# A second layer of experts in pairs of 64 rows instead of one by one with 128

## The reference, cut to what matters

```python
def moe_ffn(h, w_router, e_bias, w_gate, w_up, w_down, s_gate, s_up, s_down):
    scores = jax.nn.sigmoid(h @ w_router)                  # 64 experts
    _, idx = lax.top_k(scores + e_bias, 8)                 # 8 per token
    wts = jnp.take_along_axis(scores, idx, axis=-1)
    wts = wts / wts.sum(-1, keepdims=True) * 2.5
    ...
    # for each expert e, over the tokens that chose it:
    a = jax.nn.silu(xb @ w_gate[e]) * (xb @ w_up[e])       # 1024 -> 256
    y = a @ w_down[e]                                      # 256 -> 1024
    ...
    return routed + (jax.nn.silu(h @ s_gate) * (h @ s_up)) @ s_down
```

## Time and profile before

| | |
|---|---|
| median of 3 runs | 3581.51 us (3578.46 to 3589.11) |
| span of the profiled execution | 3580.4 us |
| its own time | not listed apart; the median is 1.1 us over the span |
| PE busy | 3395.6 us, 95% |
| DVE, ACT, POOL busy | 79%, 43%, 19% |
| mean granted TensorE clock | 0.979 of 2.4 GHz |
| traffic | 799.48 MB, mean 223 GB/s |
| second layer's experts | from about 2884 us to 3525 us of the span |

### The profile page before, as it was taken

The page is one execution under the profiler, slowest core; times in us unless marked ns, Lnnn a source line. Parts: engine busy times, 40 slices in busy tenths (PEclk is TensorE's granted clock), DMA queues, the critical chain, the costliest instruction groups (busy, mean ns, idle before and its releaser), DMA issues.

```text
span 3580.4 us, 55190 instructions
## 1 busy us (share of the span) xinstructions
PE 3395.6 (95%) x22040; PEld 2848.9 (80%) x22040; DVE 2823.8 (79%) x3225; ACT 1553.3 (43%) x2135; POOL 666.3 (19%) x437
## 2 busy tenths in 40 slices
PE   8998899999997999999899999999899899999997
PEld 8996689999995799997556777777687777777776
DVE  7877777888877777976668888888674688888885
ACT  1013323000014232011334888888432468888883
POOL 0001100101002000100002444443100024444430
PEclk9999999999998999999999999999999999999999
DMA  6545333554545344541026999999742279999993
GB/s 238 188 168 212 142 130 142 189 189 179 185 160 213 120 156 161 188 154 71 24 94 219 384 380 370 368 370 380 276 192 106 83 264 347 350 353 343 348 352 145
DMA packets 121585, 799.48 MB, mean 223 GB/s; under 512 B 34016, under 2 KB 36064, under 8 KB 51680
## 3 DMA queue, kind: packets, MB, share of 16 engines
q1 hardware_dynamic: 80208, 735.14, 55.1%
q0 software_dynamic: 39024, 59.61, 4.7%
q10 hardware_dynamic: 2080, 1.05, 0.1%
HBM read 808.77 MB, written 71.83 MB: 246 GB/s over the span
## 4 chain that ended last, share of the span: by engine, by line
PE 80%; DVE 14%; ACT 3%; DMA 2%; issue 1%; SPq 0%; DVEq 0%; POOL 0%; ACTq 0%; POOLq 0%
PE ps L453 75%; PE ps L472 4%; DVE ring_r L400 2%; DVE ring_r L399 1%; DVE ring_r L418 1%; DMA ring<-yd_dram 1%; DVE ring L1391 1%; DVE arena L2339 1%; DMA arena<-yd_dram 1%; DVE arena L1264 0%; DVE arena L1242 0%; ACT arena L1504 0%; ACT ring_r L412 0%; DVE arena L1221 0%; DVE arena L1249 0%
## 5 line engine op out<-in xcount | busy, mean ns | idle before, releaser
L453 PE MATMUL ps<-arena_r,ring_r 128*128 128x256 f32 (+1 forms) x9776 | 1278.9, 289 | 36.9 <-DVE ring_r L400 16.0
L453 PEld LDWEIGHTS ps<-arena_r,ring_r 128*128 128x128 f32 x9776 | 1218.0, 190 | 73.2 <-DVE ring_r L400 16.1
L453 PE MATMUL ps<-ring_r,arena_r 128*128 128x512 f32 (+1 forms) x2906 | 805.8, 392 | 1.3 <-DVE arena_r L2208 0.9
L453 PEld LDWEIGHTS ps<-ring_r,arena_r 128*128 128x128 f32 x2906 | 527.6, 189 | 113.7 <-DVE arena_r L2208 1.3
L453 PE MATMUL ps<-arena_hi,arena_r 128*128 128x512 f32 x1540 | 507.8, 397 | 4.7 <-DVE ring_r L2941 4.7
L400 DVE TENSOR_TENSOR ring_r<-ring,ring_r 128x4096 fp32r<-128x4096 f32 (+2 forms) x104 | 445.4, 4283 | 3.6
L3057 POOL DMA_INDIRECT yd_dram<-arena,small x129 | 229.7, 1781 | 727.4 <-PE ps L472 643.1
L453 PEld LDWEIGHTS ps<-arena_hi,arena_r 128*128 128x128 f32 x1540 | 290.1, 188 | 69.5 <-DVE ring_r L2941 5.1
L2916 DVE TENSOR_TENSOR ring_r<-ring,ring_r 128x2048 fp32r<-128x2048 f32 x130 | 298.0, 2292 | 22.8 <-ACT ring_r L2980 15.7
L2916 DVE TENSOR_TENSOR ring_r<-ring,arena_hi 128x2048 fp32r<-128x2048 f32 x128 | 293.5, 2293 | 24.3 <-ACT arena_hi L2980 17.5
L3049 POOL DMA_INDIRECT arena<-xd_dram,small x129 | 272.8, 2114 | 151.3 <-DVE arena L2737 60.7
(11 more groups left out here) (350 smaller groups left out, 3539.9 us busy)
## 6 DMA issues: line engine op xcount, KB each, us to landing
ring<-wexp_dram SPq DMA_DIRECT2D x387, 1024.0 KB, 8.8
ring<-stream_dram SPq DMA_DIRECT2D x143, 2048.0 KB, 7.8
ring<-yd_dram SPq DMA_DIRECT2D x5, 2048.0 KB, 12.7
arena<-yd_dram SPq DMA_DIRECT2D x3, 2048.0 KB, 13.4
arena<-yd_dram SPq DMA_DIRECT2D x8, 512.0 KB, 6.3
ring<-yd_dram SPq DMA_DIRECT2D x8, 512.0 KB, 9.4
xd_dram<-arena POOLq DMA_DIRECT2D x6, 512.0 KB, 6.0
consts_sb<-consts_dram SPq DMA_DIRECT2D x1, 2242.0 KB, 16.2
```

The costliest lines, as they stand in the source:

```text
L453: return pe.e.matmul(ps, lhsT=lhsT, rhs=rhs, start=start, stop=stop, skip_group_check=True)
```

## The change

Layer 1's experts are taken two at a time with 64 slots each. Blocks are now 64 slots (`SLOTS[1] = 64`), section 0 is blocks 0 to 66, always computed (64 experts and up to three second blocks), which is 33 pairs and a single block.

- The weights are no longer split: hidden and down layers are plain fp32 matmuls with a stationary operand of 64 columns, expert h of the pair in array columns 64h to 64h + 63 and PSUM rows 64h to 64h + 63 of one bank. The loops alternate h.
- Rows are not fetched from DRAM. `h` is kept in SBUF by token, as high and low parts (`HTH`, `HTL`), and PE multiplies them with a one-hot matrix of slots (`OHG`): for a group of four blocks 8 chunks x 2 token halves x 2 parts, of 256 columns (`pe_gather`), which comes out already turned.
- Results do not go to DRAM. They are scaled by their slot's weight, split into high and low (`PYH`, `PYL`), and PE multiplies them with the turned one-hot matrix (`OHT`) and adds them up in the four banks `routed`, on top of the shared expert's output, over all pairs (`combine`: 8 chunks x 2 parts, of 256 columns).
- The list of tokens, the indirect DMAs of POOL, the copies into `yd`, and the loads and sums of the combine are gone for this layer. The blocks past 64 are listed by DVE during the first three pairs (`dve_extra_experts`, `dve_extra_slots`).
- There are ten weight buffers (`NPAIR`); the issue points are six, two, then `shared`.
- Within a pair's step PE runs `hidden(j)`, `down(j-1)`, 2 transposes, half a group's gather, 2 transposes of the one-hot matrix, `combine(j-1)`. These use four banks in turn (4 to 7).

```diff
-SLOTS = {0: 128, 1: 128}
-SECTIONS = {0: ((0, 65), (65, 68), (68, 96)), 1: ((0, 64), (64, 65), (65, 68), (68, 80))}
+SLOTS = {0: 128, 1: 64}
+SECTIONS = {0: ((0, 65), (65, 68), (68, 96)), 1: ((0, 67), (67, 71), (71, 96))}
 NBLK = 96
 NRAW = 8
+NPAIR = 10
...
+        class Pairs:
...
+                self.pairs = [(b, min(2, b1 - b)) for b in range(b0, b1, 2)]
+                self.groups = [(b, min(4, b1 - b)) for b in range(b0, b1, 4)]
...
+                for j in range(len(self.pairs) + 1):
+                    if j < len(self.pairs):
+                        self.items += [(part, j, h) for part in "ab" for h in range(self.pairs[j][1])]
+                    if j:
+                        self.items += [("d", j - 1, h) for h in range(self.pairs[j - 1][1])]
...
+        def pe_gather(pe, S, g, quarters):
+            K, n = S.key, 64 * S.groups[g][1]
+            for c2 in quarters:
+                ps = take(pe, K, "gather", g, c2)
+                for c in (2 * c2, 2 * c2 + 1):
+                    o = 256 * (c % 2)
+                    for tk in range(2):
+                        for i, part in enumerate((HTH, HTL)):
+                            pe.wait_ge(*at("rows low", tk, c // 4))
+                            pe.wait_ge(*at(K, "onehot", g))
+                            ins = mm(pe, ps[:, o:o + n], as_r(part.v(1024 * tk + 128 * c, 128)), onehot(OHG, g, tk, n, True),
+                                     tk == 0 and i == 0, tk == 1 and i == 1)
+                ins.then_inc(*pe.mark("ps", K, "gather", g, c2))
+        def pe_pairs(pe, S):
+            K, np_, ng = S.key, len(S.pairs), len(S.groups)
+            pe.banks, pe.taken = range(4, 8), 0
+            if S.b0:
...
+            def hidden(j):
+                ps = take(pe, K, "hidden", j)
+                for k in range(KT):
+                    part = "a" if k < 4 else "b"
+                    for h in range(S.pairs[j][1]):
+                        pe.wait_ge(*at("left", K, "gather", j // 2, k // 2))
+                        pe.wait_ge(*S.got(part, j, h))
+                        ins = mm(pe, ps[64 * h:64 * h + 64, :], gathered(j // 2, k, 128 * (j % 2) + 64 * h, 64),
+                                 S.raw(part, j, h)[:, col(k % 4, 512)], k == 0, k == KT - 1)
+                        if k % 4 == 3:
+                            ins.then_inc(*pe.mark(K, "used", part, j))
+                pe.here("ps", K, "hidden", j)
+            def down(j):
+                for nn in range(2):
+                    ps = take(pe, K, "y", j, nn)
+                    for k in range(2):
+                        for h in range(S.pairs[j][1]):
+                            o = 1024 * k + 512 * nn
+                            pe.wait_ge(*at("left", K, "h", j))
+                            pe.wait_ge(*S.got("d", j, h))
+                            ins = mm(pe, ps[64 * h:64 * h + 64, :], PAT[j % 2].v(128 * k + 64 * h, 64), S.raw("d", j, h)[:, o:o + 512],
+                                     k == 0, k == 1)
+                            if k == 1:
+                                ins.then_inc(*pe.mark("ps", K, "y", j, nn))
+                pe.here(K, "used", "d", j)
+            def turn_hidden(j):
+                P_ = 64 * S.pairs[j][1]
+                ps = take(pe, K, "h", j)
+                for k in range(2):
+                    pe.wait_ge(*at("left", K, "hidden", j))
+                    ins = tr(pe, ps[:, 128 * k:128 * k + P_], PSUM_.v(128 * k, 128)[0:P_, :], P_)
+                ins.then_inc(*pe.mark("ps", K, "h", j))
...
+            def turn_onehot(j):
+                P_ = 64 * S.pairs[j][1]
+                ps = take(pe, K, "w", j)
+                for tk in range(2):
+                    pe.wait_ge(*at(K, "onehot", j // 2))
+                    ins = tr(pe, ps[0:P_, col(tk)], OHW[j // 2 % 2].v(256 * tk + 128 * (j % 2), P_))
+                ins.then_inc(*pe.mark("ps", K, "w", j))
+            def combine(j):
+                P_ = 64 * S.pairs[j][1]
+                for c in range(KT):
+                    for part in (PYH, PYL):
+                        pe.wait_ge(*at(K, "onehot turned", j))
+                        pe.wait_ge(*at("left", K, "y", j, c // 4))
+                        ins = mm(pe, bank("routed", c // 2)[:, col(c % 2, 256)], as_r(part[j % 2].v(128 * c, 128))[0:P_, :],
+                                 as_r(OHT[j % 2].v())[0:P_, :], False, False)
+                ins.then_inc(*pe.mark(K, "combined", j))
+            for j in range(np_ + 1):
+                if j < np_:
+                    hidden(j)
+                if j:
+                    down(j - 1)
+                if j < np_:
+                    turn_hidden(j)
+                    if j // 2 + 1 < ng:
+                        pe_gather(pe, S, j // 2 + 1, (2 * (j % 2), 2 * (j % 2) + 1))
+                    turn_onehot(j)
+                if j:
+                    combine(j - 1)
...
+        def dve_onehot(dve, S, g):
+            K, (b, n) = S.key, S.groups[g]
+            for tk in range(2):
+                hit = v3(onehot(OHG, g, tk, 64 * n, True), 64)
+                if g >= 2:
+                    dve.wait_ge(*at("ps", K, "gather", g - 2, 3))
+                    dve.wait_ge(*at("ps", K, "w", 2 * g - 3))
+                else:
+                    dve.wait_ge(*at("rows low", 1, 1))
+                dve.next.tensor_tensor(hit, counted_row(n), slots_of(RANK[tk].v(b, n), n), ALU.is_equal).then_inc(*dve.mark())
+                dve.next.tensor_tensor(v3(onehot(OHW, g, tk, 64 * n), 64), hit.bitcast(F32), slots_of(WGT[tk].v(b, n), n),
+                                       ALU.mult).then_inc(*dve.mark())
+            dve.here(K, "onehot", g)
...
+        def dve_pairs(dve, S):
+            K, np_, ng = S.key, len(S.pairs), len(S.groups)
+            def gated(j):
+                P_ = 64 * S.pairs[j][1]
+                a = PSUM_.v(0, 256)[0:P_, :]
+                dve.wait_ge(*at(K, "silu", j))
+                dve.next.tensor_tensor(a, a, bank(K, "hidden", j)[0:P_, 256:512], ALU.mult).then_inc(*dve.mark("left", K, "hidden", j))
+            def low(j, nn):
+                P_ = 64 * S.pairs[j][1]
+                lo, hi = [as_r(part[j % 2].v(512 * nn, 512))[0:P_, :] for part in (PYL, PYH)]
+                dve.wait_ge(*at(K, "y high", j, nn))
+                dve.next.scalar_tensor_tensor(lo, bank(K, "y", j, nn)[0:P_, :], slot_weight(j)[0:P_, :], hi.bitcast(F32), ALU.mult,
+                                              ALU.subtract).then_inc(*dve.mark("left", K, "y", j, nn))
+            def turned(j):
+                P_ = 64 * S.pairs[j][1]
+                of = bank(K, "w", j)[0:P_, 0:256]
+                dve.wait_ge(*at("ps", K, "w", j))
+                dve.next.tensor_reduce(slot_weight(j)[0:P_, :], of, AX.X, ALU.add).then_inc(*dve.mark(K, "weighted", j))
+                if j >= 2:
+                    dve.wait_ge(*at(K, "combined", j - 2))
...
+        def act_pairs(act, S):
+            K, np_, ng = S.key, len(S.pairs), len(S.groups)
+            def silu(j):
+                P_ = 64 * S.pairs[j][1]
+                act.wait_ge(*at("ps", K, "hidden", j))
+                if j:
+                    act.wait_ge(*at("ps", K, "h", j - 1))
+                act.next.activation(PSUM_.v(0, 256)[0:P_, :], bank(K, "hidden", j)[0:P_, 0:256], ACT.Silu, bias=0.0,
+                                    scale=1.0).then_inc(*act.mark(K, "silu", j))
+            def high(j, nn):
+                P_ = 64 * S.pairs[j][1]
+                act.wait_ge(*at("ps", K, "y", j, nn))
+                act.wait_ge(*at(K, "weighted", j))
+                if j >= 2:
+                    act.wait_ge(*at(K, "combined", j - 2))
+                act.next.activation(as_r(PYH[j % 2].v(512 * nn, 512))[0:P_, :], bank(K, "y", j, nn)[0:P_, :], ACT.Copy, bias=0.0,
+                                    scale=slot_weight(j)[0:P_, :]).then_inc(*act.mark(K, "y high", j, nn))
+            def turned(j):
+                P_ = 64 * S.pairs[j][1]
+                act.wait_ge(*at("ps", K, "h", j))
+                if j >= 2:
+                    act.wait_ge(*at(K, "used", "d", j - 2))
+                act.next.copy(PAT[j % 2].t(128)[:, :, 0:P_], v3(bank(K, "h", j)[:, 0:256], 128)[:, :, 0:P_]).then_inc(*act.mark("left", K, "h", j))
+            if S.b0:
+                for c2 in (0, 2):
+                    act_gather_out(act, S, 0, c2)
+            for j in range(np_ + 1):
+                if j < np_:
+                    silu(j)
...
+        def sp_pairs_section(sp, S):
+            l, b0 = S.l, S.b0
+            eng = Engine(sp, None, at, False)
+            for i, (part, j, h) in enumerate(S.items):
+                if i >= NPAIR:
+                    was = S.items[i - NPAIR]
+                    eng.wait_ge(*at(S.key, "used", was[0], was[1]))
+                elif not b0:
+                    c0 = first_shared[l]
+                    eng.wait_ge(*(at("released", c0 - 1) if i < 6 else at("released", c0) if i < 8 else at("shared", l)))
```

(50 more changed lines are left out.)

303 lines of the change are left out of this document (269 added, 34 removed).

## The result

The changed kernel takes 3413.78 us (median of 4 runs, 3409.9 to 3418.55) against 3579.99 us for the one before, run on the same chip: a ratio of 0.9527, with a 95% interval of 0.9514 to 0.9541. That is 166 us faster. The forecast was 3420 us in a range from 3390 to 3495, faster with a chance of 0.92. It was right; two terms of its sum were not, with errors of opposite sign. The profiled execution took 3413.98 us with a span of 3412.2 us, so 1.8 us lie outside the span.

A forecast was written before the change was run, and what follows sets the result against it. DMAs at 400 GB/s were taken as the bound: 193 loads in 506 us end at 3387, plus 7 for the last block and 25 of tail give a 3419 span, 3420 us; PE's 503 us is hidden. Range 3390 to 3495.

The forecast's parts named there:

- The pair on PE: PE's matmuls for two experts: 10.27 + 3.84 + 0.44 + 0.30 = 14.85 us a pair.
- full overlap from the four-strip rows: Hidden and down layers: array halves run side by side, as four column strips did before; 10.27 us a pair, not 20.5.
- the halves take turns: Rival, hidden and down layers: no overlap, 10.27 us more in each of 33 pairs, time 3747 us; chance 6%.
- The change between halves and whole array: PE, twice a pair: switching tiling costs 0.15 us each; bounds nothing and a whole record, 0.59.
- the bound moves to the DMAs: Expert weight loads: at 400 GB/s a pair's loads take 15.7 us, longer than PE's 14.85.
- The burst of four loads that gave 416: Trace of before: four of these loads issued together ran at 416 GB/s, upper witness for the 400 taken.
- the mixed stretches: First layer's experts, rows and scatter mixed in: 374 GB/s average, 396 to 407 at best, lower witness for the 400.
- PE would wait about 1 us a pair for loads: Sign of being right, in the pairs: PE waits for weight loads about 1 us a pair.
- The rival with 349 or 358 GB/s: Rival, weight loads: DMAs hold less; 580 us of loads and 3494 at 349, or 3479 at 358; chance 7%.
- the branch past the two unused sections lies under the last pair: End of the layer: the branch is hidden under the last pair, leaving 25 us from last combine to end.
- The chain of the engines: Before combine(j-1): ACT scaling, DVE splitting and signals take 1.6 us under 2.3 us of other PE work, costing nothing.
- Ten buffers: Weight buffers, 1.7 pairs: freed ones are needed 19 to 24 us later, enough to keep the load queue filled.

The follow-up runs named there:

- the kernel with the halves in turn: Changed kernel with loops in hidden and down swapped, so the first expert's steps all precede the second's: 3587.7 us, ratio to before 1.0007.
- two kernels: Changed kernel with ACT's scaled copy of a pair's second-half down result made three times: 3447.7 us; changed kernel without low parts in gather and combine: 3406.8 us.
- the early branch: Changed kernel with the branch moved ahead of PE's last combine and DVE's last differences: 3404.0 us, then 3407.7 against 3411.0 us side by side.

## Why the prediction was right, step by step

| term (us, if not marked) | predicted | measured, in the profile |
|---|---|---|
| first pair starts | 2879 | 2876.0 |
| pair on PE | 14.85 | 14.86 |
| PE's section | 503 | 503.8 |
| DMAs' rate | 400 GB/s, the bound | 421 GB/s, level with PE |
| section ends | 3394 | 3379.8 |
| tail | 25 | 32.4 |
| span | 3419 | 3412.2 |

**The pair on PE** is right to 0.01 us, and nearly so by its parts: 10.46 for hidden and down with the change back (predicted 10.27 + 0.15), 1.99 and 2.09 for gather and combine (1.92 each, the combine with a change of strips), 0.32 for the four transposes (0.44). That the sum agrees to a hundredth is luck, since the parts' small errors cancel. The step that carried the gain, full overlap from the four-strip rows, is shown by the kernel with the halves in turn. The price that the rival "the halves take turns" gave for its failure, 10.27 us a pair, was too high for that kernel: it assumed no overlap at all, and with the halves in turn 5.19 were lost.

The change between halves and whole array came to at most 0.19 us (10.46 less 24 steps of 0.428) and 0.17 (2.09 less the 1.92 that sixteen more matmuls took), against 0.15 taken. The Trainium skill, TensorEngine Tiling (Array Packing), Key Properties, has the drain without a figure. The trace fits a small one, but doesn't isolate it: the gather, which changes nothing between halves and whole, is 0.07 us over its 1.92 too.

**Which resource bounds** is the step that failed: "the bound moves to the DMAs", at 400 GB/s. The rate was mis-sized by 5%. The burst of four loads that gave 416 was the better witness than the mixed stretches: at 416 the 193 loads are 486 us and the last block is done at 2881 + 486 + 7 = 3374, ahead of PE's 3382, so the sum itself would have named PE. Loads alone do even better, 421. At that rate the two limits tie (14.94 and 14.86), and the end is PE's, 20 us after the last load. With it the section's end was forecast 14 us too late, 3 of them from the start. The sentence that PE would wait about 1 us a pair for loads was wrong: none. The rival with 349 or 358 GB/s is out. The Trainium skill, DMA: Bandwidth & Descriptors, Where 436 GB/s comes from, has about 358 GB/s from DRAM for a core, half of what a stack gives two cores. Here the kernel used one core, which held 421, and the measurement decides.

**The tail** is the other step that failed: "the branch past the two unused sections lies under the last pair". In PE's program the branch comes behind the last combine, and in DVE's behind the last difference. It was priced at nothing, and the changed kernel's profile has 8.2 us more there than the kernel without it. By PE's rows these are 6.02 us more ahead of the mean's matmuls (6.56 for 0.54), 0.47 more in them (3.57 for 3.10) and 1.73 more in the thirty-two behind them (5.57 for 3.84), at a granted clock of 0.50 to 0.62 for 1.00. The 6.56 are 3.2 us from the last combine to the end of PE's branch at 3383.0 and 3.4 behind it, most of them between the first weight load and its matmul. DVE's 2.7 us of "issue" behind its own branch run beside that: its first sum starts 2.0 us after the last combine. Without the branch the tail is 24.2 us, for which 25 were forecast.

**Start** was 3 us too late, within what executions differ by. The two big errors had opposite signs, -14 and +7, and that the time came out within 0.2% is luck in part. Against the parts of the gain (12 start, 117 pace, 32 end), the profile has 16, 128 and 25.

**The chain of the engines** was said to have 2.3 us of cover for 1.6 us, so 0.7 to spare; two kernels measured 0.46 and 0.54. It binds at the bank turn and not at the combine, which the prediction did not see. **Ten buffers** were called enough, and are, by the rate that stays at 421 GB/s when PE asks for more; that "enough" begins above six was not worked out.

## What to carry to other kernels

When a change makes one resource faster, work out the time of the next one as carefully as that of the first: here the pair fell to 14.86 us on TensorE and 14.94 on the DMAs, and hardly more can be had from either alone. For side-by-side experts in the array's column halves, turns of up to four records of plain fp32 are as good as strict alternation, and runs of 8 and 16 lose part of the overlap. Judge a wait by the starts of the rows and not by idle time alone: a step that has lost its partner in the other half still counts as busy. A branch at the end of a stage that sits on the engine's last work is not free: put it where matmuls are queued (3 us here by the medians), and look at its COMPARE_BRANCH record and at what stands behind it.

## What the hardware showed beyond that

- PE's taken branch lasted 3.3 to 3.8 us in all eleven profiles that have it, ACT's 0.05, and DVE's 0.06 with 2.7 us of unexplained "issue" behind it in the changed kernel's. Advanced Engine Details and Errata in the Trainium skill, Control Flow Timing, gives a compare-and-branch about 108 ns; the trace disagrees for PE by a factor of thirty. The branch jumps over two whole sections of code. That the new code has to be fetched is likely, and the DMA queues that the profile calls "instruction" speak for it. From 3.8 us before the end of the last combine to 8.2 behind it, they move in the changed kernel:

```profile
q8 instruction: 3, 0.05, 1.8%
q14 instruction: 3, 0.02, 0.8%
```

  and in the kernel without the branch:

```profile
q8 instruction: 1, 0.02, 0.5%
```

  One packet of the first kind moves at 3380.2, inside PE's branch, which ends 2.8 us later, and one at 3383.6, 2.8 us before the first of the sixteen matmuls. Which engine a packet is for the profile doesn't say, so it stays likely and is not shown.
- After the last combine the granted clock fell, to 0.68, 0.50 and 0.50 of 2.4 GHz:

```profile
3380.00:3384.00 4.00, 0.00 (x0) 0.29 (x1) 2.01 (x6) 0.21 (x1) 0.00 (x0) 0.68 0.05 10
3384.00:3388.00 4.00, 1.62 (x8) 1.62 (x8) 0.80 (x3) 0.00 (x0) 0.00 (x0) 0.50 0.02 4
3388.00:3392.00 4.00, 2.56 (x13) 2.27 (x12) 1.90 (x4) 1.20 (x2) 0.00 (x0) 0.50 0.00 0
```

  It stayed at 1.00 in the kernel without the branch, and fell in the two profiles of the early branch too (0.58 and 0.70 from 3380 to 3384), where PE's idle time was as short as without it. So the hole alone is not the cause, and what is, stays open.
- With six buffers the DMA share read 0.98 to 1.00 at 397 to 404 GB/s and with ten 1.01 at 421: a share near 1 hides 5% of the rate.
